# A hybrid decoder trunk on one core: heads of the attention in another order, the softplus sums folded on VectorE and ScalarE

## What is computed

```python
for l in range(2):
    h = rmsnorm(x, mix_norm_g[l])
    a_b, a_c, a_x, s_u, s_v, q, k, v, gates = split(h @ w_in[l])      # 1024 -> 7168 columns
    ya = a_b * causal_conv3(a_c * a_x)                                 # 512 channels
    yb = gelu(s_u) * (tril(W_s) @ layernorm(gelu(s_v)) + b)            # chunks of 128 tokens
    # attention, 8 heads of 64, rmsnorm on q and k, per head:
    z = q @ k.T / 8
    after = exclusive sum over later keys of log_sigmoid(-z)           # below the diagonal
    yc = where(mask, exp(log_sigmoid(z) + after), 0) @ v
    x = x + sum(sigmoid(gate_i) * (y_i @ w_branch_out_i)) @ w_o[l]
    x = x + (silu(g) * u) @ w_down[l]      # g, u = rmsnorm(x) @ w_gate_up[l], 2816 columns
```

## Time and profile before

| | us |
|---|---|
| median of three runs (lowest to highest) | 1672.76 (1672.59 to 1673.02) |
| the profiled execution | 1673.66 |
| its span, first to last instruction | 1671.9 |
| busy: TensorE, VectorE, ScalarE, POOL | 1662.9, 949.4, 752.4, 190.6 |

### The profile page before, as it was taken

One profiled execution on the slowest core, in us unless ns is written; L12 is line 12 of the kernel. 1 busy time (PEld: TensorE's weight loads), 2 busy tenths in 40 slices (PEclk: granted clock), 3 DMA queues, 4 the chain that ended last, 5 costly groups with the idle time before them and its releaser, 6 DMA issues.

```text
span 1671.9 us, 22070 instructions
## 1 busy us (share of the span) xinstructions
PE 1662.9 (99%) x7608; PEld 1386.7 (83%) x7608; DVE 949.4 (57%) x1172; ACT 752.4 (45%) x1059; POOL 190.6 (11%) x177
## 2 busy tenths in 40 slices
PE   8999999999999999999999999999999999999999
PEld 7888888888888888888888888888888888888887
DVE  6887876545554434434549877765555544344344
ACT  6677676333353222222456777763333432232231
POOL 0333311000020000000133233200001200000000
PEclk9999999999999999999999999999999999999999
DMA  5222222233233233233343122222323232232233
GB/s 190 84 81 88 88 76 82 89 100 100 94 101 100 89 101 100 89 101 100 113 127 101 64 88 88 88 70 96 98 90 110 89 101 96 93 100 100 89 100 126
DMA packets 49153, 162.20 MB, mean 97 GB/s; under 512 B 5712, under 2 KB 5968, under 8 KB 49104
## 3 DMA queue, kind: packets, MB, share of 16 engines
q1 hardware_dynamic: 46512, 157.08, 28.8%
q10 hardware_dynamic: 2592, 4.49, 0.7%
HBM read 155.26 MB, written 2.10 MB: 94 GB/s over the span
## 4 chain that ended last, share of the span: by engine, by line
PE 94%; DVE 2%; ACT 1%; DVEq 1%; POOLq 0%; POOL 0%; issue 0%; DMA 0%; ACTq 0%
PE bank L504 28%; PE bank L505 28%; PE bank L508 28%; PE z L577 2%; PE z L505 1%; PE z L508 1%; PE z L504 1%; PE z L550 1%; PE misc L593 1%; PE misc L591 1%; PE z L551 1%; DVE S L1321 0%; DMA par<-in_params 0%; PE bank L632 0%; DVE N L1198 0%
## 5 line engine op out<-in xcount | busy, mean ns | idle before, releaser
L504 PE MATMUL bank<-xg_hi,w_hi 128*128 128x512 f32 x1584 | 620.0, 391 | 0.0
L505 PE MATMUL bank<-xg_lo,w_hi 128*128 128x512 f32 x1584 | 616.8, 389 | 0.0
L818 ACT ACTIVATE w_hi<-raw 128x1024 fp32r<-128x1024 f32 (+1 forms) x294 | 303.5, 1035 | 483.8 <-DMA raw<-in_w_units 483.0
L1186 DVE TENSOR_TENSOR w_lo<-raw,w_hi 128x1024 fp32r<-128x1024 f32 (+1 forms) x294 | 371.2, 1265 | 42.1 <-ACT w_hi L818 21.8
L508 PE MATMUL bank<-xg_hi,w_lo 128*128 128x512 f32 x1584 | 391.7, 389 | 0.0
L508 PEld LDWEIGHTS bank<-xg_hi,w_lo 128*128 128x128 f32 x1584 | 297.4, 188 | 61.7
L504 PEld LDWEIGHTS bank<-xg_hi,w_hi 128*128 128x128 f32 x1584 | 297.5, 188 | 61.0
L505 PEld LDWEIGHTS bank<-xg_lo,w_hi 128*128 128x128 f32 x1584 | 297.5, 188 | 60.6
L1191 DVE TENSOR_TENSOR S<-bank,rstd 128x512 f32<-128x512 f32 x152 | 104.9, 690 | 267.0 <-PE bank L508 266.4
L504 PE MATMUL bank<-mid_hi,w_hi 128*128 128x512 f32 x474 | 184.6, 390 | 0.0
L505 PE MATMUL bank<-mid_lo,w_hi 128*128 128x512 f32 x474 | 184.4, 389 | 0.0
(11 more groups left out here) (200 smaller groups left out, 1675.9 us busy)
## 6 DMA issues: line engine op xcount, KB each, us to landing
raw<-in_w_units SPq DMA_DIRECT2D x278, 512.0 KB, 3.3
raw<-in_w_units SPq DMA_DIRECT2D x19, 256.0 KB, 2.9
xT<-in_x SPq DMA_DIRECT2D x8, 256.0 KB, 6.7
mix_hi<-yb_hi ACTq DMA_DIRECT2D x8, 256.0 KB, 2.3
mix_lo<-yb_lo ACTq DMA_DIRECT2D x8, 256.0 KB, 2.4
out_x<-xT SPq DMA_DIRECT2D x7, 256.0 KB, 3.9
ln_g<-in_sgu_ln_g SPq DMA_DIRECT2D x2, 256.0 KB, 4.2
ln_b<-in_sgu_ln_b SPq DMA_DIRECT2D x2, 256.0 KB, 5.0
```

The costliest lines, as they stand in the source:

```text
L504: mm(dst[:, :], wh[:, k0 + k, :], his[k], start=(k % per == 0), stop=False)
L505: mm(dst[:, :], wh[:, k0 + k, :], los[k], start=False, stop=False)
L818: af(w_hi[at.slot(c)][:, 0:kc, :], raw[at.slot(c)][:, 0:kc, :], ACT.Copy).then_inc(hi_done, 1)
L1186: tt(w[:, 0:kc, :], r[:, 0:kc, :], h[:, 0:kc, :].bitcast(F32), ALU.subtract).then_inc(lo_done, 1)
```

## The change

1. **Order.** The first scores of the next pair and its unit 0 come ahead of the second attend. Attend of the first head moves behind unit 4, scores of the second head ahead of it; the squares of k move up from behind unit 4 to behind unit 3. ScalarE and VectorE follow with their parts: the softplus of the next pair now ends the pair, `attention_exp` of the second head stands behind `ya_round`, and on VectorE the convolution stands ahead of `mixed`.
2. **Fold.** `suffix` on POOL is gone. ScalarE copies the upper 64 partitions of t_s, columns 512 to 1280, down (`fold_halves`), VectorE adds the lower ones and the later blocks (`fold_sums`), ScalarE rounds (`fold_round`), VectorE puts the low part on the upper 64 partitions (`fold_lo`). One matmul with ones then adds both parts.
3. **POOL** keeps its work of stage P and of the squares of x; in the pairs ScalarE and VectorE take the squares of q and k and the low part of k.
4. **Start.** The first half unit is issued by SyncE behind the first slice of x, not by ScalarE ahead of the parameters. The descriptor scratch that the program reserves is set to `dynamic_dma_scratch_size=4096`; the tiles `fold` and `fold_hl` (3 KB each per partition) are new.

```diff
@@ SyncE, start
             load_x(0)
+            load_half(0, 0)
             load_x(1)
@@ ScalarE, start
-            act.dma_start(raw[0][:, 0:4, :], first_units[0][:, 0:4, :]).then_inc(first_in[0], 16)
             act.dma_start(par[:, :], params[0]).then_inc(par_in, 16)
@@ TensorE, cumulate
+                later = {0: slice(0, 3 * P), 1: slice(4 * P, 6 * P), 2: slice(3 * P, 4 * P)}
                 pe.wait_ge(sp_lo, h3 + 3)
                 pe.wait_ge(suf_ok, nth + 1)
...
+                        for s in (s_hi, s_lo):
+                            last = mm(z[g][:, at:at + width], neg_tri[:, :], s[:, S_AT[i]:S_AT[i] + width],
+                                      start=False, stop=(s is s_lo and i == 3), skip_group_check=True)
+                        if i < 3:
+                            last = mm(z[g][:, at + P:at + width], neg_ones[:, :], fold_hl[:, later[i]],
+                                      start=False, stop=True, skip_group_check=True)
@@ TensorE, pair
-                    head_squares(m0 + 1, l * 8 + (j * 2 + 3))
+                    head_squares(m0 + M_SQ, heads + 3)
                     unit(at, 3, xh, xl)
-                    attend(h3, m0 + 2, pairs + 1, 0)
+                    head_squares(m0 + M_SK, heads + 4)
                     scores(h3 + 3, pairs, 1)
                     unit(at, 4, xh, xl)
-                    head_squares(m0 + 3, l * 8 + (j * 2 + 4))
+                    attend(h3, m0 + M_E0, pairs + 1, 0)
                     unit(at, 5, xh, xl)
-                    mix(m0 + 4, j, (pairs + 1) * 32, l + 1)
+                    mix(m0 + M_MIX, j, (pairs + 1) * 32, l + 1)
                     unit(at, 6, xh, xl)
-                    cumulate(h3 + 3, l * 8 + j * 2 + 1)
+                    cumulate(h3 + 3, heads + 1)
                     unit(at, 7, xh, xl)
-                    attend(h3 + 3, m0 + 5, pairs + 1, 1)
+                    scores(h3 + 6, pairs + 1, 0)
+                    unit(pl["A"](j + 1), 0, xh, xl)
+                    attend(h3 + 3, m0 + M_E1, pairs + 1, 1)
@@ ScalarE
+            def fold_halves(h3):
+                act.wait_ge(sp_ok, h3 + 3)
+                af(fold[0:HD, :], t_s[HD:P, T:1280], ACT.Copy).then_inc(fold_up, 1)
+            def fold_round(nth):
+                act.wait_ge(fold_sum, nth + 1)
...
+                af(fold_hl[0:HD, :], fold[0:HD, :], ACT.Copy).then_inc(fold_hi, 1)
+            def head_square(n_raw, src):
+                act.wait_ge(qk_raw, n_raw)
...
+                af(S2[:, :], src[:, :], ACT.Square)
+                af(sq_hi[:, :], src[:, :], ACT.Square).then_inc(qk_sq_hi, 1)
@@ VectorE
+            def fold_sums(nth):
+                half = slice(0, HD)
+                dve.wait_ge(fold_up, nth + 1)
...
+                tt(fold[half, :], fold[half, :], t_s[half, T:1280], ALU.add)
+                dve.drain()
+                tt(fold[half, 5 * P:], fold[half, 5 * P:], fold[half, 3 * P:4 * P], ALU.add)
+                dve.drain()
+                tt(fold[half, P:3 * P], fold[half, P:3 * P], fold[half, 4 * P:], ALU.add)
+                dve.drain()
+                dve.sem_inc(fold_sum, 1)
@@ VectorE, ahead of the pairs of a layer
+                softplus_sum(l * 24)
+                fold_sums(l * 8)
+                scaled(pl["A"](0), 0, N0[:, :])
+                dve.drain()
+                dve.sem_inc(v_raw, 1)
+                softplus_lo(l * 24)
```

## The result

The changed kernel takes 1707.77 us (1706.89 to 1710.79), the kernel before on the same chip 1672.89: a ratio of 1.0207, 95% interval 1.0194 to 1.0220, or 34.9 us more. The prediction was 1693.0 with a range of 1665 to 1712. The direction and the mechanism hold, the size is 14.8 us short: the time lies above the 1683 to 1705 of the forecast with waits as laid out, and only rival 3 (the clock) reaches it. The profiled execution of the changed kernel took 1706.89 us (span 1705.2).

What follows compares the result with a forecast made beforehand. TensorE's matmuls were taken to bound the kernel before. Two layers at +10.3 us each (4.15 + 7.5 - 1.3, matmul savings included) less 0.4 for the start gave +20.2: 1693.0 us on the median, range 1665 to 1712.

Steps and rivals of the forecast that it cites:

- forecast with waits as laid out: Whole kernel: TensorE waits for the lengthened VectorE and ScalarE chains as calculated; 1683 to 1705 us, chance 0.58.
- rival 3: TensorE's clock falls at up to eight waits, up to 19 us on top: 1697 to 1712; chance 0.14 beyond 1705.
- Matmuls removed: TensorE's cumulates: 11 matmuls instead of 16, 1.61 us instead of 2.28; sixteen cumulates save 10.7 us.
- Start: Kernel start: the parameters' DMA is issued one issue earlier, so ScalarE's first matmul operand comes sooner; -0.4 us.
- The fold's length: Behind the softplus: ScalarE's copy 0.84 us, VectorE's adds 0.95, 0.29 and 0.42 plus drains; together 2.8 us.
- First pair: First pair of each layer: TensorE's transposes wait 4.15 us, since VectorE reads v behind the fold.
- The steady pair: Cumulate to next cumulate, link by link: 59.2 us, then 59.6, against 57.5 and twice 56.7; +7.5 us a layer.
- (a): Steady pair, cumulate to mix: ScalarE and VectorE links reach the attention output add at 22.2 us; mix waits 0.4.
- (b): Steady pair, mix to scores: links reach the end of the second head's exps at 37.2 us; scores wait 1.0.
- (c): Steady pair, scores to transposes: links reach the output add that frees misc at 53.2 us; transposes wait 2.3.
- Rivals 1 and 2: Chains shorter than laid out: by 4 us a period, 1660.5 us, chance 0.13; by 2 us, 1681, chance 0.13.
- rival 1: TensorE stays the bound, nothing waits: 1660.5 us, or 1668.8 with only two waits of 4.15; chance 0.13.

Runs made afterwards that it cites:

- e9: Changed kernel, reordered only: v read and misc freed ahead of the fold, second-head exps, softplus logs and sums, q's bank read earlier; 1666.26 us, ratio 0.9955.
- e6: Kernel before, in its old order, with only the fold and 11-matmul cumulates in place of POOL's suffix; 1702.64 us, ratio 1.0171.
- e1: Changed kernel, but VectorE reads v ahead of the softplus sums and fold in a layer's first pair; 1702.75 us, ratio 1.0175.
- e3: Changed kernel, but ScalarE does the second head's exps ahead of ya's rounding and split 9; 1715.07 us, ratio 1.0251.
- e2: Changed kernel, but inside the loop everything that frees the bank misc goes ahead of the fold; 1686.48 us, ratio 1.0078.
- e4: Changed kernel's order, start and squares, but without the fold: POOL's suffix and 16 matmuls a cumulate as before; 1674.44 us, ratio 1.0004.

## Why the prediction was right in direction and short in size

**Matmuls removed: right.** A cumulate is 1.62 us for the 1.61 predicted, and e9 shows the period of 55.5. The saving was real and stayed unseen, since TensorE waited.

**Start: under-sized.** The first matmul starts at 7.52 and not 8.56, and the first scores 0.85 us earlier (predicted 0.4).

**The fold's length: nearly right.** Copy 0.84, adds 0.95, 0.28 and 0.42, as costed; from the end of the sums to the end of the drains 3.0 us for the 2.8.

**First pair: right, but for the clock.** Wait 4.04 us for 4.15. Behind it come 1.4 us at the low clock.

**The steady pair: the right four waits at the right places, each too small.** Measured against predicted: mix 1.0 and 0.56 for 0.4, scores 1.27 for 1.0, transposes 2.4 for 2.3. These listed waits look close; the lateness is greater than they say, since a matmul's modelled end (0.39 us) lies 0.17 behind the time at which the next could have started. In positions from the cumulate, in the first pair of layer 0: mix at 22.6 for 22.2, scores at 38.1 for 37.2, transposes at 54.5 for 53.2, the next cumulate at 60.5 for 59.2. The terms that were mis-sized are (a), (b) and (c): I added the durations of the links, with a drain here and there. Each of the three stretches came out 0.4 to 0.5 us longer. The rows' own durations are as costed; the excess is between them: 0.2 in each fold, some 0.2 ahead of the norm chain of k, and 0.1 to 0.25 from the end of the row that releases TensorE to its matmul. That is 1.15 us a period (those of the later pairs were put at 59.6), 3.4 a layer.

**Rival 3, the clock, came on top of the forecast.** I had it as a case for itself with 0.14, at up to eight places of 2.3 us. It happened at four of the eight, at 1.4 us each, 5.7 us in all. The step that failed is treating it as an alternative to the waits and not as a part of their price. The price was taken from the start, where the stretch had lasted longer.

The sum on the profiled execution: 20.2 predicted; + 5.7 for the clock, + 6.9 for six longer periods, - 0.45 for the start, gives +32.4, and +33.2 was measured (1706.89 less 1673.66); 0.8 stays unexplained. The rest to 34.9 is how the two profiled executions stand to their medians.

**Rivals 1 and 2** (the chains overlap more than I could see) fell in the changed kernel, and so did my expectation of e6 that the old order would hide the fold, at least where I had put it. But rival 1's world is nearly reachable by order alone: e9 took 1666.3 us, where rival 1 gave 1660.5, and its last period has no wait. Of rival 1's counter-argument, the work of VectorE (some 50 us) was put too high; 47 was measured, and it was not the sum of work that decided.

## What to carry to other kernels

Work taken from the bound engine and given to two idle-looking ones (here 44.6 and 41.2 of 56.7 us) must be costed at its place in their mutual chain: here each fold delayed the release of a shared bank, and 10.7 us of matmuls were bought with 44 us of waits and slow stretches. When a wait is moved, see whether it disappears or turns up at the next link (e1, e3), and if it turns up, look for the gap in which the late engine itself stands idle, and fill that one (e9). Release shared banks ahead of long work that doesn't need them; that alone gave 21 of the 41 us, and the fold of e6 stood ahead of such a release once more.

## What the chip showed that I had not expected

- **The clock falls after waits of some 2 us already, though not each time.** In the profiled executions of this study a stretch at 1.2 GHz followed all eighteen waits of 2.69 to 4.1 us in the pairs (changed kernel, e2, e3, e6), twelve of the thirty-two between 1.7 and 2.6 us, and none of the shorter ones. The same wait of 2.4 us was followed by it in the second pair of a layer of the changed kernel and not in the first and third. The two that were measured cost 1.4 us each. Neither count is a rule: two executions of e6, whose profiled one has six waits of 2.7 to 2.9 us, show no fall at all, and there the six cost about 1 us together. The Trainium skill, "TensorE: Matmul & The Clock Gate", section Why this matters for your kernels, warns of gaps between bursts; as I had read it, only the waits of 4 us would count. The rows above show one of 2.38 us that did.
- **POOL's two-input instructions cost VectorE more than their own length.** Three subtractions went from 1.62 to 3.96 and 4.41 us beside POOL work (3.98 in the kernel before already), two that take 1.39 together to 3.02. A VectorE that keeps the work (e4: 42.70 us a pair against 44.57) is less busy than one that shares it.
